# Order of VectorE's and ScalarE's work around heads, variances and routing's exponentials, with small loads split and the last sums copied by token half

## The reference, cut to what matters

```python
for l in range(DEPTH):
    hn = rmsnorm(x, norm1_g[l])
    q, k, v, hy_in, gates = split(hn @ w_in[l])              # 512,512,512,1536,2048 columns
    q, k = rmsnorm(q per head), rmsnorm(k per head)
    a_out = neighbourhood_attention(q, k, v, na_rpb[l])      # 8 heads, softmax with bias and mask
    u = short_conv(hy_in, hy_conv_w[l], hy_conv_b[l])        # width 3, per channel
    h_fwd, h_bwd = hyena_filters(...)                        # sin(sin(pos @ w1) @ w2) @ w3, times a decay
    b_out = hyena_mixer(u, h_fwd, h_bwd, hy_bias[l])         # long convolution by Fourier products
    merged = g0 * (a_out @ w_up_na[l]) + g1 * (b_out @ w_up_hy[l])   # g = sigmoid(gates + gate_b)
    x = x + merged @ w_out[l]
    x = x + peer(rmsnorm(x, norm2_g[l]), peer_wq[l], peer_subkeys[l], peer_u[l], peer_v[l])
```

## Time and profile before

| what | value |
|---|---|
| median of 3 runs | 2057.78 us (2057.1 to 2058.68) |
| the profiled execution | 2058.63 us, of it 2056.8 us from the first to the last instruction (span) |
| TensorE busy | 2030.8 us (99% of the span), 13628 matmuls |
| ScalarE, VectorE, GpSimd busy | 1071.0, 1253.2, 1603.5 us |
| granted TensorE clock | 9 or more tenths in all 40 slices of the page |
| loads over the span | 356.49 MB read, 174 GB/s on average |

### The profile page before, as it was taken

How to read it: one execution, slowest core, us unless ns; L and a number is a source line. 1 busy time by engine, 2 the same in 40 slices (tenths; PEclk the granted TensorE clock), 3 DMA queues, 4 the chain that set the end, 5 groups by cost and what they waited for, 6 DMA issues and landing times.

```text
span 2056.8 us, 44277 instructions
## 1 busy us (share of the span) xinstructions
PE 2030.8 (99%) x13628; PEld 1816.6 (88%) x13628; DVE 1253.2 (61%) x2621; ACT 1071.0 (52%) x2288; POOL 1603.5 (78%) x1316
## 2 busy tenths in 40 slices
PE   8999999999999999999999999999999999999999
PEld 7988999998888888888888899999988888888887
DVE  6586479778888333333375763896788873333333
ACT  6553554554444555555565545545444445555554
POOL 6766878887777788888877768788877778888886
PEclk9999999999999999999999999999999999999999
DMA  9433545554444555555584435455544445555554
GB/s 279 154 135 122 205 154 184 184 170 147 153 151 145 184 194 194 193 191 193 197 234 151 137 132 199 161 179 179 173 144 153 153 143 192 192 191 192 193 193 152
DMA packets 102816, 358.39 MB, mean 174 GB/s; under 512 B 11680, under 2 KB 16738, under 8 KB 102244
## 3 DMA queue, kind: packets, MB, share of 16 engines
q1 hardware_dynamic: 102036, 355.14, 51.3%
q10 hardware_dynamic: 720, 2.44, 0.3%
HBM read 356.49 MB, written 1.05 MB: 174 GB/s over the span
## 4 chain that ended last, share of the span: by engine, by line
PE 60%; POOL 22%; issue 16%; POOLq 1%; ACT 1%; DVE 0%; DMA 0%; SPq 0%; DVEq 0%; ACTq 0%
PE bank L1730 34%; POOL w_lo L394 22%; PE bank L1659 12%; PE bank L1661 6%; PE bank L1670 4%; PE bank L1368 1%; PE bank L1372 1%; PE bank L1370 1%; POOLq L392 0%; DMA ring<-stream 0%; DVE raw_lo L837 0%; ACT w_hi L457 0%; POOLq L415 0%; ACT raw_hi L508 0%; PE bank L1754 0%
## 5 line engine op out<-in xcount | busy, mean ns | idle before, releaser
L394 POOL TENSOR_TENSOR w_lo<-ring,w_hi 128x512 fp32r<-128x512 f32 x1048 | 1403.3, 1355 | 360.4 <-ACT w_hi L457 360.0
L457 ACT ACTIVATE w_hi<-ring 128x512 fp32r<-128x512 f32 x1312 | 753.6, 621 | 378.0 <-PE bank L1372 368.2
L394 DVE TENSOR_TENSOR w_lo<-ring,w_hi 128x512 fp32r<-128x512 f32 x256 | 236.5, 924 | 452.5 <-ACT w_hi L457 452.4
L1368 PE MATMUL bank<-act_parts,w_hi 128*128 128x256 f32 x1600 | 458.9, 287 | 1.8 <-POOL w_lo L394 1.8
L1370 PE MATMUL bank<-act_parts,w_hi 128*128 128x256 f32 x1600 | 452.7, 283 | 0.0
L1372 PE MATMUL bank<-act_parts,w_lo 128*128 128x256 f32 x1600 | 452.6, 283 | 0.0
L1730 PE MATMUL bank<-w_hi,e_hi 128*128 128x512 f32 x1024 | 398.9, 390 | 2.1 <-DVE arena L1307 1.9
L1730 PE MATMUL bank<-w_hi,e_lo 128*128 128x512 f32 x1024 | 398.4, 389 | 0.0
L1730 PE MATMUL bank<-w_lo,e_hi 128*128 128x512 f32 x1024 | 398.4, 389 | 0.0
L1659 PE MATMUL bank<-act_parts,w_hi 128*128 128x512 f32 x1088 | 385.9, 398 | 0.0
L1368 PEld LDWEIGHTS bank<-act_parts,w_hi 128*128 128x128 f32 x1600 | 306.7, 192 | 10.8 <-issue 7.0
(11 more groups left out here) (214 smaller groups left out, 2400.2 us busy)
## 6 DMA issues: line engine op xcount, KB each, us to landing
ring<-stream SPq DMA_DIRECT2D x656, 512.0 KB, 3.2
arena<-rpb_in SPq DMA_DIRECT2D x8, 512.0 KB, 8.8
arena<-dft_in SPq DMA_DIRECT2D x2, 1024.0 KB, 8.4
arena<-subkeys ACTq DMA_DIRECT2D x2, 1024.0 KB, 5.6
xT<-x_in SPq DMA_DIRECT2D x4, 256.0 KB, 6.7
arena<-w_in SPq DMA_DIRECT2D x2, 512.0 KB
arena<-decay_in SPq DMA_DIRECT2D x2, 512.0 KB
out<-xT SPq DMA_DIRECT2D x4, 256.0 KB, 2.3
```

Of the source, the lines that this page charges most:

```text
L394: eng.tensor_tensor(w_lo[:, part_, :], ring[:, tile % RING, half * HT:(half + 1) * HT], w_hi[:, part_, :].bitcast(F32), ALU.subtract).then ...
L457: nc.scalar.activation(w_hi[:, 2 * (tile % AHEAD) + half, :], ring[:, tile % RING, half * HT:(half + 1) * HT], ACT.Copy).then_inc(hi_ready ...
L1368: T.matmul(out_, weights(w_hi, tile, j), hi[:, k, :], start=start, stop=False, skip_group_check=True)
```

## The change

- **Small loads.** `net_in` now counts four loads (w1, pos, ffn_col, w2). A new signal `taps_in` counts spread, w3, skip and decay, which are issued among the refills of tiles 4 to 8. The mask and `dft` are moved from between tiles 4 and 6 to behind the last piece of bias, ahead of the refill of tile 12.
- **Variances.** ScalarE splits tile 11 (`tile_wait(T_V + 1)`) before it takes the root. VectorE sums w3 after the second sine argument.
- **Heads.** VectorE does `conv` 0 to 3 before the first normalisation (two before the first scores, two behind the second), and the rest in a new order. ScalarE does the exponentials of heads h + 1 and h + 2 around odd heads h.
- **Routing's exponentials.** Their table is loaded before tile 122 (`T_U + 50`) is split, and they come behind that split. Gelu's table is loaded by the next gelu.
- **Last gelus.** The last two go to banks 2 and 3 (`last_fresh`), so that the first `peer_v` tile waits for two fewer of `late_stored`.
- **The end.** Bank 6 is copied as soon as its own three products are done (`early_sum`), bank 7 in two halves, and `final_turns` transposes by token half.

```diff
@@ layer_loads (SyncE)
-                small(net_in, w3, w3_in[at].rearrange("a p b n -> (a p) b n"))
-                small(net_in, skip[0:1, :], skip_in[at, :])
-                small(net_in, decay[:, :, :], decay_in)
-                small(net_in, spread, spread_in)
                 refill(l * GROUPS + 1, 0)
-                small(tables_in, mask, mask_in)
+                small(taps_in, spread, spread_in)
                 refill(l * GROUPS + 1, 1)
-                small(tables_in, dft[:, :, :, :], dft_in)
+                small(taps_in, w3, w3_in[at].rearrange("a p b n -> (a p) b n"))
                 for slot in range(2, RING):
                     refill(l * GROUPS + 1, slot)
+                small(taps_in, skip[0:1, :], skip_in[at, :])
+                small(taps_in, decay[:, :, :], decay_in)
                 for r in range(ROWS):
                     refill(l * GROUPS + 2, r % RING)
                     offsets(r)
+                small(tables_in, mask, mask_in)
+                small(tables_in, dft[:, :, :, :], dft_in)
@@ variances and heads (ScalarE)
                 tile_wait(T_V)
+                tile_wait(T_V + 1)
                 act.wait_ge(qk_var_ready.sem, qk_var_ready.at(l, 1))
                 root(qk_tmp, rms_ps, P, qk_root.sem)
-                tile_wait(T_V + 1)
...
+                    if h % 2 and h + 1 < NH:
+                        head_exp(h + 1)
                     gate(2 * h + 1)
-                    if h + 2 < NH:
+                    if h % 2 and h + 2 < NH:
                         head_exp(h + 2)
@@ routing's exponentials (ScalarE)
                 gelus(0, SORTED - RING)
+                load_table(ACT.Exp)
+                high_parts(l, 0, T_U + SORTED - RING + AHEAD)
                 act.wait_ge(best_ready.sem, best_ready.at(l, 1))
                 nc.scalar.activation(expd[:, :, :], expd[:, :, :], ACT.Exp).then_inc(expd_ready.sem, 1)
-                load_table(ACT.Gelu_apprx_tanh)
-                gelus(SORTED - RING, ROUTED - SORTED + RING)
+                gelu(0, SORTED - RING)
+                for n in range(SORTED - RING + 1, SORTED):
+                    high_parts(l, 0, T_U + n + AHEAD)
+                    gelu(0, n)
+                gelus(SORTED, ROUTED - SORTED)
@@ heads (VectorE)
+                conv(0)
+                conv(1)
+                head_scores(0)
+                head_scores(1)
+                conv(2)
+                conv(3)
+                tiles = [4, 8, 5, 9, 6, 10, 7, 11]
+                normalise_probs(0)
+                for p in range(NH // 2):
+                    if p:
+                        dve.wait_ge(pv_done.sem, pv_done.at(l, p))
+                        V.tensor_copy(attn_T[:, p - 1, :], bank[7][:, 0:S]).then_inc(attn_ready.sem, 1)
+                    if tiles:
+                        conv(tiles.pop(0))
+                    normalise_probs(2 * p + 1)
+                    if tiles:
+                        conv(tiles.pop(0))
+                    if p + 1 < NH // 2:
+                        head_scores(2 * p + 2)
+                        head_scores(2 * p + 3)
+                        if tiles:
+                            conv(tiles.pop(0))
+                        if p == 2:
+                            V.tensor_tensor(zT[:, :, :], u[:, 4:8, :], u[:, 8:12, :], ALU.mult
+                                            ).then_inc(z_ready.sem, 1)
+                        normalise_probs(2 * p + 2)
@@ first peer_v tile, last tile and end (TensorE)
-                            pe.wait_ge(late_stored.sem, late_stored.at(l, LATE))
+                            pe.wait_ge(late_stored.sem, late_stored.at(l, LATE - AHEAD))
...
+                    if last and half and tt == 0:
+                        ins.then_inc(early_sum.sem, 1)
...
+            def final_turns(l):
+
+                for tt in range(TT):
+                    for b in (2, 3):
+                        if tt == 0:
+                            pe.wait_ge(sum_by_act.sem, sum_by_act.at(l, 2))
+                        else:
+                            pe.wait_ge(sum_by_dve.sem, sum_by_dve.at(l, b))
+                        for j in range(2):
+                            at = j * S + tt * P
+                            ins = T.transpose(delta[b][:, at:at + P],
+                                              v_out[:, 2 + tt, (2 * b - 4 + j) * P:(2 * b - 3 + j) * P], identity)
+                        if tt:
+                            ins.then_inc(delta_done.sem, 1)
```

More of the change, by code:

```diff
@@ L216, in encoder_kernel @@
         fresh = [bank[6 + n][:, 0:S] for n in range(2)]
+        last_fresh = [bank[2 + n][:, 0:S] for n in range(2)]
         cols_in = sem("cols_in")
@@ L222, in encoder_kernel @@
         x_loaded = [sem(f"x_loaded{b}") for b in range(KT // 2)]
[L223 removed]
+        net_in = sig("net_in", 16 * 4)
+        taps_in = sig("taps_in", 16 * 4)
         tables_in = sig("tables_in", 16 * (2 + ROWS))
@@ L727, in act_layer, with gelu @@
                                          ).then_inc(score_copied.sem, 1)
+                def gelu(i, n):
+                    nc.scalar.activation(experts[:, bass.ds(i * RING + n, 1), :].rearrange("p a t -> p (a t)"),
+                                         bank[n % 2][:, 0:S], ACT.Gelu_apprx_tanh).then_inc(gelu_done.sem, 1)
                 def gelus(first, count):
@@ L732, in gelus @@
                             high_parts(l, i, T_U + first + s + AHEAD)
-                            nc.scalar.activation(experts[:, bass.ds(i * RING + (first + s), 1), :].rearrange(
-                                "p a t -> p (a t)"), bank[s % 2][:, 0:S], ACT.Gelu_apprx_tanh
-                                ).then_inc(gelu_done.sem, 1)
+                            gelu(i, first + s)
                 def expert_high(i, n):
@@ L795, in sum_copy @@
             def sum_copy(l, half, tt):
-                if half:
+                if half and l == DEPTH - 1:
+                    act.wait_ge(early_sum.sem, early_sum.at(l, 1))
+                elif half:
                     act.wait_ge(tile_done.sem, tile_done.at(l, TILES))
@@ L912, in sine_argument, with sum_copy @@
                                     ).then_inc(arg_ready.sem, 1)
-                def sum_copy(half):
-                    if half:
-                        dve.wait_ge(tile_done.sem, tile_done.at(l - 1, TILES))
-                    else:
-                        dve.wait_ge(v_sum.sem, v_sum.at(l - 1, 1))
-                    V.tensor_copy(v_out[:, 2 * half + 1, :], bank[5 + 2 * half][:, :]).then_inc(sum_by_dve.sem, 1)
+                def sum_copy():
+                    dve.wait_ge(v_sum.sem, v_sum.at(l - 1, 1))
+                    V.tensor_copy(v_out[:, 1, :], bank[5][:, :]).then_inc(sum_by_dve.sem, 1)
                 def x_pair(b):
@@ L938, in dve_layer @@
                 if l == DEPTH:
-                    sum_copy(0)
+                    sum_copy()
                     add_delta(0, x_pair(0))
                     add_delta(1, x_pair(1))
-                    sum_copy(1)
+                    dve.wait_ge(tile_done.sem, tile_done.at(l - 1, TILES))
+                    for j in range(2):
+                        V.tensor_copy(v_out[:, 3, j * S:(j + 1) * S], bank[7][:, j * S:(j + 1) * S]
+                                      ).then_inc(sum_by_dve.sem, 1)
                     add_delta(2, x_pair(2))
@@ L1002, in dve_layer @@
                 sine_argument(2, 2)
+                dve.wait_ge(taps_in.sem, taps_in.at(l, taps_in.per_layer))
+                V.tensor_tensor(w3_sd[:, 0, :], w3[:, 0, :], w3[:, 1, :], ALU.add)
+                V.tensor_tensor(w3_sd[:, 1, :], w3[:, 0, :], w3[:, 1, :], ALU.subtract
+                                ).then_inc(w3_ready.sem, 1)
                 for n in range(4):
@@ L1052, in head_scores, with normalise_probs @@
                                     ).then_inc(scores_ready.sem, 1)
-                head_scores(0)
-                head_scores(1)
-                tiles = [4, 8, 5, 9, 6, 10, 7, 11, 0, 1, 2, 3]
-                for h in range(NH):
+                def normalise_probs(h):
                     dve.wait_ge(exp_done.sem, exp_done.at(l, h + 1))
```

41 lines of the change are left out of this document (15 added, 26 removed).

## The result

| | before | changed |
|---|---|---|
| median of 13 runs | 2057.92 us (2057.1 to 2059.51) | 2063.14 us (2059.2 to 2067.98) |
| the profiled execution | 2058.63 us, span 2056.8 | 2061.39 us, span 2059.6 |
| ratio of the runs | | 1.0022 (95% interval 1.0015 to 1.0029) |

The change makes the kernel 5.2 us slower, above the forecast of 2054.6 and above its range, which ended at 2058.6. Two things are worth seeing at once. And almost everything that the forecast hoped for did happen; it is the loads that cost more than all of it.

A forecast was written before the change was run, and what follows sets the result against it. TensorE, busy 2030.8 of 2056.8 us, was taken as the bound. Terms -5.8 + 4.45 - 0.95 - 0.4 - 0.5 = -3.2 us gave 2054.6 us beside the median of 2057.78, range 2049.7 to 2058.6.

The forecast's parts named there:

- The moved tables: At tile 12's first product: mask and dft ahead of it delay its landing 2.85 us, costing +4.45 us over both layers.
- rival 1: At tile 12: the moved mask and dft cost nothing and it lands as before, giving 2049.7 us; chance 0.15.
- rival 3: After tile 12's waits TensorE comes back slow, 2.8 us per event, giving 2060.2 to 2062 us; chance 0.09.
- Heads: At the heads' transposes: TensorE's six waits for VectorE's normalised probabilities go, -5.8 us.
- Routing: At the product after the routing's exponentials: half the 0.88 us wait stays, for gelu 48; -0.48 us per layer.
- Last gelus: At peer_v: the first tile's 0.95 us wait goes, the second waits for expert 1's low part; -0.2 us per layer.
- Variances: At v's products around tile 11: splitting before the root, and moving w3's sums, gains 0, bounds -0.9 and 0.
- The end: At the last additions: bank 7's half copies let the first add start earlier, -0.5 us, bounds 0 and -0.8.
- the loads' term: The cost of moving mask and dft ahead of tile 12, +4.45 us, bounds 0 and +7.8.

The follow-up runs named there:

- all_parts: Changed kernel with each bias piece replaced by 512 KB of the stream, written as 4 rows of 1 KB on all 128 partitions: 2049.23 us.
- taps_back: Changed kernel with w3, skip, decay and spread back ahead of tile 4, mask and dft left behind the last bias piece: 2057.68 us.
- tables_late: Changed kernel with w3, skip, decay and spread ahead of tile 4, and mask and dft behind tile 13: 2051.18 us.
- loads_back: Changed kernel with SyncE's loads in the order of before, all other engines' orders still changed: 2050.36 us.
- heads_only: Kernel before with only the heads' new order on VectorE and ScalarE: 2053.22 us, ratio 0.997.
- bias_late: Changed kernel with small loads, mask and dft at their old places, and the four bias pieces behind tiles 7, 9, 12 and 14: 2049.07 us.
- long_rows: Changed kernel with each bias piece replaced by 512 KB of the stream in 4 KB rows on 128 partitions: 2049.33 us.
- before_bias_late: Kernel before with only the four bias pieces spread out, behind tiles 7, 9, 12 and 14: 2057.4 us, ratio 0.999.
- tables_back: Changed kernel with only mask and dft back around tile 5, the small loads still split among tiles 4 to 8: 2054.51 us.
- same_rows: Changed kernel with each bias piece replaced by 512 KB of contiguous stream, written to the same 64 partitions in 1 KB rows: 2063.72 us.

## Why the prediction was wrong, step by step

- **The small loads: the step that failed, because it was not there.** The forecast put a price on the mask and `dft` and none on w3, skip, decay and spread, whose split the same edit brings. The 1.2 MB of these four went out at 7 to 9 us, while the ring's slots were full and the refill of tile 4 was not due until 12.6 us (timeline of SyncE, before):

```profile
8.02 0.33 SPq L335 DMA_DIRECT2D arena<-decay_in  x1
8.39 0.43 SPq L335 DMA_DIRECT2D arena<-spread_in  x1
12.61 0.33 SPq L321 DMA_DIRECT2D ring<-stream  x1
```

  Now they go out among tiles 4 to 8, tile 8 lands later, and tile 11 with it. I had read only what stands directly ahead of tile 12. Price: 4.1 us alone, 5.5 on top of the moved tables (12.8 less 7.3). In the profiled execution this is the wait of 3.65 us at tile 11, for which the forecast had nothing. The bytes themselves had been made up by 30 us; most of the loss comes up behind that, in the bias stretch, and with the pieces of bias on all partitions it is gone (all_parts). So the split costs what it does only together with the slow bias writes; how it slows them stays open.
- **Where the miss comes from.** The result lies 8.5 us above the forecast of 2054.6: 4.1 for the split, 2.7 for the clock at tile 12, 1.4 that the two load edits cost together beyond their sum, and a few tenths.
- **The moved tables: mechanism and waits right.** Forecast +4.45 us of waits at tile 12, measured +4.7 (taps_back against loads_back). The 2.85 us of delay show as about 3 us between the landings of tiles 11 and 12. Tile 12 is delayed by the tables ahead of it, so rival 1 falls. The Trainium skill, "DMA: Bandwidth & Descriptors", "Queues, rings and completion order", says that completion is not FIFO per issuing engine. The trace of tables_late agrees: the mask lands 1 us ahead of tile 13, which was issued before it.
- **The clock: rival 3, which had 0.09.** Its place (the waits at tile 12; the layer 0 event came at tile 11), size (2.8 us an event; measured 2.6 in layer 0 and 1.5 in layer 1 of the changed kernel) and time (2060.2 to 2062) were near what happened. A time above 2061.9, where the result lies, had 0.05. I had read it off the slow start behind the first 9 us, and was misled by the row of the granted clock, which says 1.00 there. The products tell otherwise. Those of the kernel before at 14 us stand 0.21 us apart:

```profile
13.91 0.41 PE L1370 MATMUL bank<-raw_lo,w_hi 128*128 128x256 f32 x1
14.12 0.41 PE L1372 MATMUL bank<-raw_hi,w_lo 128*128 128x256 f32 x1
```

and so do those of the changed kernel in layer 1, where the trace does record 0.50:

```profile
1078.39 0.41 PE L1397 MATMUL bank<-act_parts,w_hi 128*128 128x256 f32 x1
1078.60 0.42 PE L1399 MATMUL bank<-act_parts,w_hi 128*128 128x256 f32 x1
```

  At 2.4 GHz they are 0.12 apart. The record of the clock begins only where the slow start ends (15.0 us in the execution of before), and a stretch without a record reads 1.00. So the kernel before did show a low clock behind its first 9 us without a matmul. Against the rival I had set the waits of 1.3 us, shorter than the 2.1 and 2.8 us of my own sum; 0.09 was too little.
- **Heads.** Forecast -5.8 us, measured, matmul for matmul, -5.6 in loads_back (2.7 and 2.9) and -5.4 alone (heads_only). The working takes 1.7 us for a normalisation in its sums that it reads as 1.2 from the rows, so the even heads had nearer 2 us to spare than 1. They were not late; head 5's transposes start at 140.88, 7.5 us behind head 4's, with no wait; they were 8.87 apart:

```profile
133.39 0.66 PE L1574 MATMUL bank<-mats,arena 128*128 128x128 f32 x4
...
140.88 0.60 PE L1574 MATMUL bank<-mats,arena 128*128 128x128 f32 x4
```

- **Routing.** Forecast: half of the wait stays, for gelu 48. Measured: 0.50 us of 0.88, for L735, which is gelu 48; -0.4 a layer for -0.48. The timelines of ScalarE and of TensorE:

```profile
416.66 0.40 ACT L766 ACTIVATE arena<-arena 128x256 f32<-128x256 f32 x1
417.07 1.28 ACT L735 ACT_TABLE_LOAD   x1
418.37 0.38 ACT L735 ACTIVATE arena<-bank 128x256 f32<-128x256 f32 x1
```

```profile
418.88 0.38 PE L1397 MATMUL bank<-act_parts,w_hi 128*128 128x256 f32 x1 [0.50 <-ACT arena L735]
```

- **Last gelus.** Forecast: `e_lo` takes over and -0.2 a layer stays. Measured -0.24 at the second tile's first product, of which less than 0.1 is left a few products on (both layers, loads_back too). The wait that took over:

```profile
687.34 0.50 PE L1760 MATMUL bank<-w_hi,e_hi 128*128 128x512 f32 x1 [0.82 <-POOL e_lo L425]
```

- **Variances.** Forecast 0, bounds -0.9 and 0. In layer 0 the edit gives 0.5 us wherever the tile has landed in time: loads_back, bias_late, long_rows and all_parts gain it, heads_only and before_bias_late, which lack the edit, do not. In layer 1 loads_back gains 1.0 at the same place, where tile 11 landed 10.6 us after its issue for 11.6 before; heads_only has 0.8 of that without the edit, so most of it is the landing. In the changed kernel the wait of 1.3 us was gone there because TensorE came 4.3 us later.
- **The end.** Forecast -0.5, measured -0.9 up to the last transposes, of which 0.4 is lost again behind them. The idle time ahead of the last additions fell from 0.81 to 0.20:

```profile
2054.52 0.76 DVE L955 COPY arena<-bank 128x256 f32<-128x256 f32 x2 [0.52 <-PE bank L1760]
2055.48 1.29 DVE L940 TENSOR_TENSOR xT<-bank,xT 128x512 f32<-128x512 f32 x2 [0.20 <-PE bank L1801]
```

Without the loads' term the forecast's other terms make -7.65 us; loads_back measures 8.3 us between the two spans, and 8.9 by its ratio. Of the 8.3 the heads, routing, last gelus and end make 7.1; 1.5 come from tile 11's place in the two layers, and 0.4 were lost in the first 16 us. The sign was decided by the one edit that had no computation in it.

## What to carry to other kernels

When loads are reordered, price every load that moves, also one that moves away from the tile you look at: here 1.2 MB, taken out of a stretch in which SyncE waits for slots anyway, made tiles late that land over 30 us later. The room for such a move depends on how fast the rest of the stretch is: in this kernel, spreading the four pieces of bias out took the scatter away, and writing as many bytes to all 128 partitions at once took the whole cost away. Where a sum contains a wait longer than any in the profile at hand, give the chance that it costs more than its length a real weight.

## What the runs showed of the hardware

- Writes of 512 KB to 64 partitions are slow and slow down the tiles in flight beside them as well. From 28 to 48 us the kernels with four such writes moved 198 to 270 GB/s at a DMA share over 1.0, against 331 at 0.92 and no backlog when the same bytes in the same 1 KB rows go to 128 partitions. A tile's 4 KB packet took 222 ns for 160 (32 to 34 us).
- TensorE's clock fell to 1.2 GHz around all eight waits of 3.0 to 3.8 us and around waits of 1.9, 2.3 and 2.4 us, and stayed there for 3.4 or 6.8 us, which cost 1.3 to 2.6 us each. It stayed at 2.4 GHz behind waits of 1.5 and 1.9 us in tables_back and of 2.3 us in layer 1 of same_rows, so the length of the wait alone does not decide it:

```profile
1075.26 0.36 PE L1397 MATMUL bank<-act_parts,w_hi 128*128 128x256 f32 x1 [2.33 <-POOL w_lo L397]
```

  Its products behind that line stand 0.12 us apart. What does decide it was not settled.
- The scatter of this kernel's times has its source in these writes to 64 partitions where they stand close together: 6 us over eighteen runs on one chip as they are, 0.5 over five with the pieces spread out, and 0.4 over four with the same bytes on 128 partitions at the same places.
